# Spatial weights turned by VectorE, and a first load in smaller pieces, in a one-core hybrid decoder layer

## The reference

```python
h = rms_norm(x, pre_norm[l])
proj = h @ w_in[l]                       # (1024, 1024) @ (1024, 8448)
q, k, v, gate_a, u_b, v_b, gate_b, mg_a, mg_b = jnp.split(proj, offsets, axis=-1)
o_a = sliding_window_attention(q, k, v, sinks[l], rel_bias)
y_a = (o_a * jax.nn.silu(gate_a)) @ w_branch_a[l]
o_b = spatial_gating(gelu(u_b), gelu(v_b), sgu_ln_g[l], sgu_ln_b[l], w_spatial[l], b_spatial[l])
y_b = (o_b * jax.nn.silu(gate_b)) @ w_branch_b[l]
merged = sigmoid(mg_a) * y_a + sigmoid(mg_b) * y_b
x = x + rms_norm(merged @ w_out[l], post_norm[l])

def spatial_gating(u, v, ln_g, ln_b, w_s, b_s):      # w_s (8, 128, 128), b_s (8, 128)
    vn = layer_norm(v, ln_g, ln_b)
    vc = vn.reshape(B, nc, CHUNK, SGU_GROUPS, SGU_GROUP_DIM)
    w = jnp.where(causal[None], w_s, jnp.zeros_like(w_s))
    mixed = jnp.einsum('gts,bnsgd->bntgd', w, vc) + b_s.T[:, :, None]
    return u * mixed.reshape(B, S, SGU_WIDTH)
```

## Time and profile before

| | us |
|---|---|
| median of 3 runs (lowest, highest) | 891.44 (890.86, 891.86) |
| the profiled execution | 891.49 |
| its span, first to last instruction | 889.8 |
| busy: PE, PEld, DVE | 882.6, 740.7, 617.9 |
| busy: POOL, ACT | 543.6, 505.7 |

### The profile page before, as it was taken

The page is one execution under the profiler, slowest core; times in us unless marked ns, Lnnn a source line. Parts: engine busy times, 40 slices in busy tenths (PEclk is TensorE's granted clock), DMA queues, the critical chain, the costliest instruction groups (busy, mean ns, idle before and its releaser), DMA issues.

```text
span 889.8 us, 12481 instructions
## 1 busy us (share of the span) xinstructions
PE 882.6 (99%) x4204; PEld 740.7 (83%) x4204; DVE 617.9 (69%) x1127; ACT 505.7 (57%) x981; POOL 543.6 (61%) x404
## 2 busy tenths in 40 slices
PE   9999999999999999999999999999999999999997
PEld 7888888888888888888888888888888888888885
DVE  6866795455555554555555576978789879899968
ACT  6554355776767676767677663443444434534553
POOL 3564424888898978897979798554442252042236
PEclk9999999999999999999999999999999999999999
DMA  8895754463646476665554563653197640444004
GB/s 306 204 205 139 232 189 131 136 169 107 171 117 162 126 186 147 180 158 156 134 158 119 154 166 106 217 161 95 48 355 268 217 177 0 142 153 178 1 0 190
DMA packets 199872, 139.29 MB, mean 157 GB/s; under 512 B 91368, under 2 KB 165376, under 8 KB 199680
## 3 DMA queue, kind: packets, MB, share of 16 engines
q1 hardware_dynamic: 197568, 135.05, 51.2%
q10 hardware_dynamic: 2240, 3.43, 1.1%
HBM read 98.06 MB, written 43.54 MB: 159 GB/s over the span
## 4 chain that ended last, share of the span: by engine, by line
PE 94%; POOL 2%; DVE 1%; issue 1%; DMA 1%; ACT 0%; SPq 0%; DVEq 0%; ACTq 0%; POOLq 0%
PE acc L1047 47%; PE acc L1217 11%; PE acc L900 10%; PE ps_m L1217 7%; PE ps_t L1217 7%; PE ps_t L1064 3%; PE ps_m L1085 3%; PE acc L990 2%; POOL w_lo L1831 1%; DMA soft<-prob_d 1%; PE ps_t L930 1%; PE ps_m L930 1%; DVE c L2199 0%; POOL sums L1898 0%; SPq L676 0%
## 5 line engine op out<-in xcount | busy, mean ns | idle before, releaser
L1047 PE MATMUL acc<-mv,w_hi 128*128 128x512 f32 x1344 | 346.1, 391 | 0.3 <-DVE c L2102 0.3
L1047 PEld LDWEIGHTS acc<-mv,w_hi 128*128 128x128 f32 x1344 | 246.9, 188 | 47.6 <-issue 0.8
L1047 PE MATMUL acc<-mv,w_lo 128*128 128x512 f32 x672 | 180.1, 390 | 0.0
L1831 POOL TENSOR_TENSOR w_lo<-sums,w_hi 128x1024 fp32r<-128x1024 f32 x48 | 116.4, 2426 | 54.8 <-ACT w_hi L1382 49.8
L1047 PEld LDWEIGHTS acc<-mv,w_lo 128*128 128x128 f32 x672 | 126.1, 188 | 27.3
L1831 POOL TENSOR_TENSOR w_lo<-raw,w_hi 128x1024 fp32r<-128x1024 f32 (+1 forms) x48 | 93.8, 1954 | 32.4 <-ACT w_hi L1375 22.5
L1217 PE MATMUL acc<-right,left 128*128 128x512 f32 x432 | 98.7, 389 | 0.0
L1217 PEld LDWEIGHTS acc<-right,left 128*128 128x128 f32 x432 | 81.0, 188 | 17.2 <-DVE left L2212 0.4
L1586 ACT ACTIVATE soft<-soft,neg_max 128x129 f32<-128x129 f32 x128 | 50.5, 396 | 56.0 <-DVE neg_max L2152 55.8
L2167 DVE TENSOR_TENSOR soft<-ps_m,soft 64x256 f32<-64x256 f32 x32 | 13.3, 416 | 84.7 <-ACT soft L1619 84.7
L900 PE MATMUL acc<-mv 128*128 128x512 f32 x288 | 69.3, 394 | 0.0
(11 more groups left out here) (282 smaller groups left out, 1660.4 us busy)
## 6 DMA issues: line engine op xcount, KB each, us to landing
raw<-in_w_in SPq DMA_DIRECT2D x56, 512.0 KB, 5.3
prob_d<-soft SPq DMA_DIRECT2D x32, 256.0 KB, 4.0
soft<-prob_d SPq DMA_DIRECT2D x128, 64.0 KB, 3.0
ht_d<-sums SPq DMA_DIRECT2D x8, 512.0 KB, 4.9
mix_d<-mix_b SPq DMA_DIRECT2D x8, 512.0 KB, 3.8
ga_d<-gate SPq DMA_DIRECT2D x16, 256.0 KB, 3.4
tb<-tb_d SPq DMA_DIRECT2D x4, 1024.0 KB, 5.1
ub<-mix_d SPq DMA_DIRECT2D x7, 512.0 KB, 3.5
```

Of the source, the lines that this page charges most:

```text
L1047: ins = nc.tensor.matmul(bank, (w_lo if y == 2 else w_hi)[:, left + k * P:left + (k + 1) * P], right[:, (OPW if y == 1 else 0) + k * HALF: ...
L1831: nc.gpsimd.tensor_tensor(w_lo[:, c], src, w_hi[:, c].bitcast(f32), ALU.subtract).then_inc(wlo_ok, 1)
```

## The change

Four things. **First**, the spatial matrix: it is loaded twice, once as it lies (`w_nat`, for the row sums) and once as 32x32 squares in four DMAs of runs of 128 bytes (`wsq`); VectorE turns the squares in one instruction, GpSimd cuts the triangle of both copies, VectorE sums the rows in one reduction, and the sums go to memory and come back broadcast (`rs_d`, `rs_b`). The eight transposes and the four matmuls with ones are gone from TensorE; `row_weights` runs in two pieces in units 3 and 4. **Second**, the start: the first two row tiles of x arrive as columns 0 to 255 and then 256 to 1023, the transposes go by 2, 2 and 4 slices instead of 4 and 4, and W's tile 0 arrives in two halves with a semaphore each; six turns of the identity become three; pre_norm's load moves from SP's queue to ACT's. **Third**, positions: mixes and transposes inside the units move by some matmuls, a unit waits for the halves of its low part apart, GpSimd's bias row is made in other portions, `c_22` goes ahead of `left_sums_2`, and the first load of v comes one step earlier. **Fourth**, the end: the last half row is no longer divided; VectorE adds all 512 columns.

```diff
-XP = ((0, 0), (1, 0), (0, 1), (1, 1))
+XP = ((0, 0, 2), (1, 0, 2), (0, 2, 4), (1, 2, 4), (0, 4, 8), (1, 4, 8))
-V_PARTS = ((9, 6), (10, 1), (10, 4), (11, 0))
+V_PARTS = ((9, 5), (10, 1), (10, 4), (11, 0))
...
         @block.sync
-            sp.dma_start(pre8, pre_norm[0].rearrange("(k p) -> k p", p=P)).then_inc(small_in, 16)
-            load_vb(0)
-            sp.dma_start(x_b[1][:, 0:HALF], x[0, P:2 * P, 0:HALF]).then_inc(x1_pre_in, 16)
+            sp.dma_start(land[0][:, S1h], w_in_t[:, 0, VB_COL:VB_COL + HALF]).then_inc(w0_in, 16)
+            sp.dma_start(land[0][:, S2h], w_in_t[:, 0, VB_COL + HALF:VB_COL + D_MODEL]).then_inc(vb_in[0], 16)
+            sp.dma_start(x_b[1][:, 0:2 * P], x[0, P:2 * P, 0:2 * P]).then_inc(x1_pre_in, 16)
             load_vb(1)
+            sp.dma_start(x_b[0][:, 2 * P:], x[0, 0:P, 2 * P:]).then_inc(x_in[0], 16)
             load_vb(2)
-            sp.dma_start(x_b[0][:, HALF:], x[0, 0:P, HALF:]).then_inc(x_in[0], 16)
-            load_vb(3)
-            sp.dma_start(x_b[1][:, HALF:], x[0, P:2 * P, HALF:]).then_inc(x_in[1], 16)
-            for k in range(4, KT):
+            sp.dma_start(x_b[1][:, 2 * P:], x[0, P:2 * P, 2 * P:]).then_inc(x_in[1], 16)
+            for k in range(3, KT):
                 load_vb(k)
...
-            sp.dma_start(wsp[:, :].rearrange("p (g s) -> p g s", g=KT),
-                         w_spatial[0].rearrange("g t s -> t g s")).then_inc(wsp_in, 16)
+            sp.dma_start(w_nat[:, :].rearrange("p (g s) -> p g s", g=KT),
+                         w_spatial[0].rearrange("g t s -> t g s")).then_inc(wn_in, 16)
+            w_squares = w_spatial[0].rearrange("g (q j) (a i) -> a j (g q) i", q=4, a=4)
+            for a in range(4):
+                sp.dma_start(wsq[32 * a:32 * (a + 1), :].rearrange("j (c i) -> j c i", i=32), w_squares[a]).then_inc(wsp_in, 16)
...
-            sp.wait_ge(bmat_ok, 1)
-            sp.dma_start(bmat_d[:, :], wsp[:, :]).then_inc(wsp_in, 16)
+            sp.wait_ge(rs_ok, 1)
+            sp.dma_start(rs_d.rearrange("a (t g) -> t (a g)", t=P), w_rows[:, :]).then_inc(rs_out, 16)
...
         @block.tensor
             def mix(t):
-                    pe.wait_ge(bmat_ok, 1)
+                    pe.wait_ge(dve_made, DVE_WSL)
...
             def vb_unit(t):
-                pe.wait_ge(hs_lo, lo_count(t))
+                pe.wait_ge(hs_lo, lo_count(t) - 1)
...
-                    vb_mms(t, 0, 16)
-                    row_sums()
-                    vb_mms(t, 16, 22)
+                    vb_mms(t, 0, 22)
...
                     transpose_h(t + 1)
-                    vb_mms(t, 22, 41)
+                    vb_mms(t, 22, 44)
                     mix(0)
-                    vb_mms(t, 41, 48).then_inc(unit_done, 1)
+                    vb_mms(t, 44, 48).then_inc(unit_done, 1)
...
-            transpose_x(0, 0)
-            for _ in range(WARM_UP // 4):
+            transpose_x(0, 0, 2)
+            for _ in range(WARM_UP // 8):
...
+            vb_tile(0, 0, 1, 2)
             pe.wait_ge(dve_made, DVE_PRE)
-            transpose_x(1, 0)
-            vb_tile(0, 0, 1, 3)
+            transpose_x(1, 0, 2)
             vb_tile(1, 0, 0, 1)
+            vb_tile(0, 0, 2, 3)
             vb_tile(1, 0, 2, 3)
             vb_tile(1, 0, 1, 2)
-            vb_tile(0, 1, 0, 2)
+            vb_tile(0, 1, 0, 1)
+            transpose_x(0, 2, 4)
+            vb_tile(0, 1, 1, 2)
             vb_tile(1, 1, 0, 2)
-            transpose_x(0, 1)
             vb_tile(0, 1, 2, 3)
+            transpose_x(1, 2, 4)
             vb_tile(1, 1, 2, 3)
-            transpose_x(1, 1)
-            for k in range(2, 5):
+            vb_tile(0, 2)
+            transpose_x(0, 4, 8)
+            vb_tile(1, 2)
+            transpose_x(1, 4, 8)
+            for k in range(3, 5):
                 vb_tile(0, k)
                 vb_tile(1, k)
...
-            pe.wait_ge(made, MADE_WSP)
-            for g in range(KT):
-                c = slice(g * P, (g + 1) * P)
-                ins = nc.tensor.transpose(ps_m[:, c], wsp[:, c], ident[:, :])
-            ins.then_inc(tr_done, 1)
             vb_tile(1, 7).then_inc(unit_done, 1)
...
         @block.scalar
-            xp_hi(0, 0)
-            xp_hi(1, 0)
+            xp_hi(0, 0, 2)
+            xp_hi(1, 0, 2)
+            xp_hi(0, 2, 4)
             vb_hi(2)
+            xp_hi(1, 2, 4)
             vb_hi(3)
             square_x(0)
-            xp_hi(0, 1)
+            xp_hi(0, 4, 8)
             square_x(1)
-            xp_hi(1, 1)
+            xp_hi(1, 4, 8)
...
         @block.vector
                 if s == 2:
-                    if n >= POOL_SUMS:
-                        left_sums_2(n + 1)
...
                     c_22(n)
+                    if n >= POOL_SUMS:
+                        left_sums_2(n + 1)
...
+            dve.wait_ge(wsp_in, 64)
+            nc.vector.transpose(wsq[:, :], wsq[:, :]).then_inc(dve_made, 1)
+            dve.wait_ge(made, MADE_WN)
+            nc.vector.tensor_reduce(w_rows[:, :], k3(w_nat[:, :]), mybir.AxisListType.X, ALU.add).then_inc(rs_ok, 1)
             ln_stats(0)
+            ln_apply(0)
             dve.wait_ge(act_made, ACT_WSH)
...
-            ln_apply(0)
-            row_weights()
             h_lo(3)
```

More of the change, by code:

```diff
@@ L476, in wait_vb_lo, with hi_count @@
             eng.wait_ge(vb_lo_ok, k + 1)
+        def hi_count(t, k):
+            return [(u, j) for u, a, b in XP for j in range(a, b)].index((t, k)) + 1
         def lo_count(t):
-            return len(XL) + t - 1
+            return len(XL) + 2 * (t - 1)
         def k3(buf):
@@ L902, in vb_mms, with transpose_x @@
                 return ins
-            def transpose_x(t, half):
-                pe.wait_ge(x_in[t] if half else (x0_bs_in, x1_pre_in)[t], 16)
-                if half:
+            def transpose_x(t, first, last):
+                pe.wait_ge(x_in[t] if first else (x0_bs_in, x1_pre_in)[t], 16)
+                if first == 4:
                     pe.wait_ge(hs_lo, XL.index((t, 1)) + 1)
-                for k in range(4 * half, 4 * half + 4):
+                for k in range(first, last):
                     ins = nc.tensor.transpose(xp_ps[t][:, xp_cols(k)], x_b[t][:, k * P:(k + 1) * P], ident[:, :])
@@ L1243, in square_x, with xp_hi @@
                 nc.scalar.activation(junk if t else junk_0, x_b[t % 2 if t < 4 else 0], ACT.Square, accum_out=ssq[:, t % 2:t % 2 + 1]).then_inc(ssq_ok, 1)
[L1245 to L1247 removed]
+            def xp_hi(t, first, last):
+                act.wait_ge(x0_tr, 2 + XP.index((t, first, last)))
                 act.wait_ge(dve_made, DVE_PRE)
[L1249 to L1250 removed]
+                for k in range(first, last):
+                    nc.scalar.activation(h_dst(0, k // 4, t)[:, k % 4, :], xp_ps[t][:, xp_cols(k)], ACT.Copy,
                                          scale=pre_col[:, k:k + 1]).then_inc(hs_hi, 1)
@@ L2549, in _ @@
                     h_lo(t + 1)
+                if t == 3:
+                    row_weights(0, 3)
+                if t == 4:
+                    row_weights(3, KT)
             t_sums(0)
```

153 lines of the change are left out of this document (74 added, 79 removed).

## The result

The changed kernel takes **894.38 us** (median of 9 runs, 892.83 to 895.66), the kernel before in the same job 891.86: ratio 1.0024, 95% interval 1.0015 to 1.0034. It is slower by 2.5 us, where 1.8 gained was forecast; the time lies outside the range. The nine runs fall into two groups, 892.8 to 893.0 (three) and 894.2 to 895.7 (six), where the kernel before has one; the profiled execution, 893.04 with a span of 891.2, is of the first.

What follows compares the result with a forecast made beforehand. TensorE's instruction list, plus what precedes its first useful matmul and the tail, bounds the kernel. 891.49 with -1.78 (list), +0.5 (start), 0 (first mix), -0.3 (`c_22`), -0.15 (tail), sum -1.73, gives 889.76, stated as 889.7; range 888.2 to 891.6.

Steps and rivals of the forecast that it cites:

- I leave its transposes where they are, 4.02: Start: transposes of x's first quarter stay at 4.02 us, so the first matmul comes at 5.2, 0.96 earlier.
- the turn comes near 6 us: Start: TensorE's clock goes from 1.2 to 2.4 GHz near 6 us; the first two matmuls take about 0.45.
- the sign of being wrong that was named: One of three: slower clock beyond 7 us, start waits missing, or TensorE waiting over 0.5 us between 30 and 50.
- T: Start: the moment, 11.46 us, when TensorE is to turn tile 1's slices 2 and 3 of x.
- The two waits: Start: TensorE waits 0.38 us for ScalarE's high part of x, then 1.16 for VectorE's `vb_lo(2)`.
- The bound: Start: 36 matmuls and 16 transposes done at 16.9 against 16.25, taken as +0.5; from 0.9 earlier to 1.1 later.
- Rival 4: Start: clock stays at 1.2 GHz longer, ten more matmuls at 0.45 cost 2.2 us, giving 891.9; chance 0.05.
- Off TensorE's list: Spatial part: eight transposes (0.87 us) and four matmuls with ones (0.91) leave TensorE's list, -1.78.
- The first mix: Mix(0), near 42.4 us: no wait expected, term 0, with 1.0 us of stall as upper bound.
- The 0.6 to spare: Mix(0): GpSimd's `vn_low(0)` was to end 0.6 us before need, down from 4.0.
- The DMA queue: SP's queue: the squares' four issues take 4.86 us, landing near 31, covered by about 1 us.
- `c_22` and the tail: Near 558 us and the end: -0.3 for the `c_22` wait (to 0), -0.15 for the tail (-0.3 to +0.2).

Runs made afterwards that it cites:

- a_xfirst: Changed kernel with x's first quarter issued first on ScalarE's queue and pre_norm first on SP's: 891.49 us.
- a_all3: Changed kernel with pre_norm first on SP, x's quarter first on ScalarE's queue, VectorE's W tile 2 copy earlier, six fillers behind x's first transposes: 890.71 us.
- s_pre_act: Changed kernel with the old first load, but pre_norm issued on ScalarE's queue ahead of x's first half: 891.95 us.
- a_best: Changed kernel with thirteen fillers before x's transposes, VectorE's W tile 2 copy earlier, tile 1's first transposes ahead of tile 0's low-part matmuls: 890.45 us.
- a_lo2: Changed kernel with VectorE copying tile 2 of W ahead of the low parts of tile 1's slices 2 and 3: 892.71 us.

## Why the prediction was wrong

- **The step that failed first** is in the start: "x's first quarter is half as large but is issued behind pre_norm; I leave its transposes where they are, 4.02". They ran at 4.98. The two facts were not weighed. Half the size saves little: issued first, x's half lands 2.6 to 3.3 us after its issue and its quarter 2.5 and 2.9 (`a_xfirst`, `a_all3`). Going out behind pre_norm, and behind W's first pieces, costs more than the 0.6 of the issue: the quarter then takes 3.4 to 4.1, here 3.5, and the half 4.6 and 4.7. `s_pre_act` prices the line at 2.4 us.
- **The second** is "the turn comes near 6 us". It was read from one profile (5.8 there); with the late x it came at 8.2 in the profile and later in others, and even with the same start it varies by 2.7 us. This is the sign of being wrong that was named, the slower clock beyond 7 us; the other two did not appear. The first four matmuls took 2.02 instead of the 1.35 worked out, and T, worked out as 11.46, is 13.66: 1.1 from the later first matmul (0.96 of it x's), 0.7 from these four, 0.1 from the wait and 0.3 from the ten behind it.
- **A term put at nothing**: a wait costs more than its idle time. The ten matmuls behind the first take 2.56 at the higher clock and not 2.27, the two behind the second 0.75 and not 0.45: 0.3 for each wait.
- **The two waits were right.** For ScalarE 0.46 (worked out: 0.38), for `vb_lo(2)` 1.10 (1.16). From T to the end of the 16 transposes 5.71 (5.4; the 0.3 is that of the second wait).
- **The bound was too narrow.** The start got +3.1 against a range of -0.9 to +1.1, whose upper end let x land 0.5 late. Rival 4, the clock, had ten matmuls at 2.2 us and a chance of 0.05; the profiles show it with three to eight of them, and x late beside it.
- **Off TensorE's list** -1.78: exact. 45.04 is worked out from it and 45.03 measured.
- **The first mix.** The reduction took 1.18 (1.2), the turn 1.23; GpSimd's `vn_low(0)` 3.33 where 2.40 was taken. It ended at 44.72, 0.3 us before mix(0), though TensorE came there 2.6 later than worked out. The 0.6 to spare were an overestimate that the slow start hid (with the start mended, `a_all3` and `a_best` wait 0.4 here):

```profile
33.80 1.23 DVE L2534 STREAM_TRANSPOSE mix_b<-mix_b 128x1024 f32<-128x1024 f32 x1
34.96 1.18 DVE L2536 TENSOR_REDUCE row_sum<-mix_b 128x8 f32<-128x1024 f32 x1
...
40.13 2.32 DVE L2541 TENSOR_TENSOR ws_st<-mix_b,ws_st 128x1024 fp32r<-128x1024 f32 x1
```

```profile
41.39 3.33 POOL L1770 TENSOR_TENSOR w_lo<-ev,w_hi 128x1024 fp32r<-128x1024 f32 x1
```

- **The DMA queue** was mis-sized: the four issues of the squares took twice the 4.86 us of the earlier trace rows, and landed 7.3 us behind their issue; VectorE reached them later still, so it cost nothing here (in `a_xfirst`, with the sooner start, VectorE waited 0.36 for them):

```profile
20.92 10.10 SPq L575 DMA_DIRECT2D mix_b<-in_w_spatial  x4
```

- **`c_22` and the tail.** The wait is gone; what follows TensorE's last matmul is 5.5 us instead of 5.8. Singly neither is told from the scatter, the sum of all but the start is: 2.2 gained where 2.23 was summed. That the two agree to 0.1 is partly luck, since the parts are no better known than 0.3.
- The forecast without its start term stands to a few tenths; the term for the start was +0.5 where the profile has +3.1 and the medians of the kernels with and without it differ by 4.8. Between the two profiles the start makes 2.9 and the place near 545 us another 0.6; the rest of the 4.8 lies in executions of the upper group, of which the changed kernel has no profile.

## What to carry to other kernels

The first place among the loads is worth something: one line that put a small load ahead of the one that the critical engine waits for, and let a large one out 0.46 sooner on the other queue, cost four times its own issue time (2.4 us for 0.6). Which of its two effects counts for how much was not separated. Before cutting a first load finer, follow every engine's list through the first microseconds: moving one copy ahead in VectorE's list took the wait of 1.1 us down to 0.3 (`a_lo2`). Measure unrelated parts of a change apart; here one gained 2.2 us and the other lost 4.8, and the old load with the new rest, 889.58, beats both kernels.
